# A Strassen scheme in the down projection of a two-layer convolutional MLP

## The reference

```python
D_FF = 2816
def conv_mlp(h, w_up, conv_w, conv_b, w_down):
    S = h.shape[1]
    u = h @ w_up
    up = jnp.pad(u, ((0, 0), (CONV_WIDTH - 1, 0), (0, 0)))
    uc = conv_b + sum(conv_w[j] * up[:, j:j + S] for j in range(CONV_WIDTH))
    gate, val = jnp.split(uc, 2, axis=-1)
    return (jax.nn.gelu(gate, approximate=True) * val) @ w_down
...
    for l in range(DEPTH):
        ...
        h = rms_norm(x, norm_mlp_pre[l])
        y = conv_mlp(h, w_up[l], conv_w[l], conv_b[l], w_down[l])
        x = x + rms_norm(y, norm_mlp_post[l])
```

## Time and profile before

| | |
|---|---|
| median of three runs | 3897.62 us |
| span of the profiled execution | 3899.6 us |
| TensorE matmul busy | 3734.7 us, 96% |
| VectorE busy | 2203.4 us, 57% |
| ScalarE busy | 1471.4 us, 38% |
| GpSimd busy | 1920.5 us, 49% |
| down projection of layer 0, first to last matmul | about 2468 to 2711 us |
| down projection of layer 1 | about 3649 to 3891 us |

### The profile page before, as it was taken

The page is one execution under the profiler, slowest core; times in us unless marked ns, Lnnn a source line. Parts: engine busy times, 40 slices in busy tenths (PEclk is TensorE's granted clock), DMA queues, the critical chain, the costliest instruction groups (busy, mean ns, idle before and its releaser), DMA issues.

```text
span 3899.6 us, 49530 instructions
## 1 busy us (share of the span) xinstructions
PE 3734.7 (96%) x19015; PEld 3088.3 (79%) x19015; DVE 2203.4 (57%) x3514; ACT 1471.4 (38%) x2954; POOL 1920.5 (49%) x1675
## 2 busy tenths in 40 slices
PE   6999999899999998999898999999999898999998
PEld 5888887887888877877687888887878587888887
DVE  4425254836777756544648777444444648777533
ACT  3224231326666653226544333222225534333211
POOL 3223223823333327221536888976221526778975
PEclk9999999999999999999899999999999999999999
DMA  5323222320000013110132222544110132222543
GB/s 182 96 83 92 81 67 85 107 78 15 6 12 6 9 37 102 61 30 7 33 131 78 81 84 79 200 145 138 49 36 17 33 125 73 84 84 87 180 161 124
DMA packets 244615, 309.84 MB, mean 79 GB/s; under 512 B 38085, under 2 KB 156245, under 8 KB 244378
## 3 DMA queue, kind: packets, MB, share of 16 engines
q1 hardware_dynamic: 211768, 231.86, 19.1%
q10 hardware_dynamic: 32610, 74.80, 5.5%
HBM read 252.96 MB, written 51.53 MB: 78 GB/s over the span
## 4 chain that ended last, share of the span: by engine, by line
PE 68%; DVE 12%; ACT 3%; issue 3%; POOL 1%; DMA 0%; ACTq 0%; SPq 0%; DVEq 0%; POOLq 0%
PE ps L130 64%; PE ps L133 3%; DVE ml_p L142 3%; DVE cst_sm L153 3%; ACT thi L136 1%; DVE f_ta L150 1%; DVE f_tb L150 1%; ACT ml_o L136 1%; DVE tlo L142 1%; ACT tfi L136 0%; POOL mlo_z L142 0%; DVE cst_sm L150 0%; DVE tfl L142 0%; POOL mix_z L142 0%; DMA wst<-in_w_in 0%
## 5 line engine op out<-in xcount | busy, mean ns | idle before, releaser
L139 POOL CAST whi<-wst 128x512 fp32r<-128x512 f32 (+2 forms) x508 | 423.9, 834 | 1241.2 <-DMA wst<-in_a_w_in 347.9
L142 POOL TENSOR_TENSOR wlo<-wst,whi 128x512 fp32r<-128x512 f32 (+2 forms) x634 | 936.2, 1484 | 40.8
L130 PE MATMUL ps<-whi,thi 128*128 128x512 f32 (+3 forms) x1816 | 710.1, 391 | 28.7 <-DVE tlo L142 10.8
L130 PE MATMUL ps<-whi,tlo 128*128 128x512 f32 (+3 forms) x1816 | 686.2, 378 | 0.0
L130 PE MATMUL ps<-wlo,thi 128*128 128x512 f32 (+3 forms) x1816 | 685.6, 378 | 0.0
L130 PEld LDWEIGHTS ps<-whi,thi 128*128 128x128 f32 x1816 | 345.2, 190 | 90.5 <-DVE tlo L142 11.9
L130 PEld LDWEIGHTS ps<-wlo,thi 128*128 128x128 f32 x1816 | 345.5, 190 | 57.7 <-issue 3.8
L130 PEld LDWEIGHTS ps<-whi,tlo 128*128 128x128 f32 x1816 | 344.6, 190 | 58.3
L130 PE MATMUL ps<-thi,whi 128*128 128x512 f32 x856 | 339.2, 396 | 23.2 <-DVE tlo L142 15.0
L130 PE MATMUL ps<-thi,wlo 128*128 128x512 f32 x856 | 336.0, 392 | 0.0
L130 PE MATMUL ps<-tlo,whi 128*128 128x512 f32 x856 | 335.9, 392 | 0.0
(11 more groups left out here) (393 smaller groups left out, 8103.9 us busy)
## 6 DMA issues: line engine op xcount, KB each, us to landing
wst<-in_w_down SPq DMA_DIRECT2D x140, 256.0 KB, 3.3
wst<-in_w_up SPq DMA_DIRECT2D x126, 256.0 KB, 2.9
scr_h<-f_tb SPq DMA_DIRECT2D x44, 512.0 KB, 3.9
wst<-in_w_in SPq DMA_DIRECT2D x80, 256.0 KB, 2.8
da_am<-in_ada_w SPq DMA_DIRECT2D x64, 256.0 KB, 2.7
wst<-in_a_w_in SPq DMA_DIRECT2D x72, 192.0 KB, 2.4
f_T2lw<-scr_h SPq DMA_DIRECT2D x48, 256.0 KB, 3.8
tfl<-scr_h SPq DMA_DIRECT2D x40, 256.0 KB, 3.8
```

The source lines that it names most:

```text
L130: return self.none if self.e is None else self.e.matmul(*a, **k)
L139: return self.none if self.e is None else self.e.tensor_copy(*a)
L142: return self.none if self.e is None else self.e.tensor_tensor(*a)
```

## The change

The down projection is cut in 2 x 2 x 2 blocks: two halves of the positions, two halves of the 22 feature tiles (tiles 2 to 12, and tiles 0, 1 and 13 to 21) and two halves of the columns. A Strassen scheme (the variant of Winograd) makes seven block products out of them. A product has 11 steps `e` of one contraction tile each, and a step covers four row tiles `t` with three matmuls each. That is 77 steps of 12 matmuls, 924 matmuls in a layer. Three products accumulate in the four banks of chain `y`, two in the banks of chain `x1` and two in those of `x2`; the intermediate values of a chain are read out between the products.

The sums of operands are new. In products 1, 2 and 4 each step needs a sum of hidden tiles and a sum of weight tiles. The hidden difference `S3` is made by VectorE during the up projection (`difference`) and stored to `d_s`. `S2` is made by GpSimd (`pool_down_sum`), four steps ahead. `T3`, `T2`, `T4`, `S4`, `T1` and `S1` are made by VectorE (`dve_down_sums`), four steps ahead too. Raw tiles that are needed more than once stay in kept tiles (`keep`: 11 each of `1`, `3`, `4` and `S`). ScalarE now makes all high parts, of weights too (`act_down`). GpSimd makes the low parts of all weights and those of the hidden tiles in `POOL_LOWS`; VectorE makes the other ones. Rows 0 to 3 end with product 5 and rows 4 to 7 with product 6, the last.

The core of the diff:

```diff
+    DOWN = [("A11", "B11", "x1"), ("S2", "T2", "y"), ("A12", "B21", "x1"), ("S3", "T3", "y"), ("S1", "T1", "x2"),
+            ("A22", "T4", "y"), ("S4", "B22", "x2")]
...
+    def down_h_free(self, l, e):
...
+        return self.S.at("tile", ("dw", l, e - 8))
...
+        for e in range(6, 12):
+            self.sp_feature(sp, l, e)
+        for i in range(4):
+            self.sp_keep(sp, l, "S", i)
+            self.sp_keep(sp, l, "S", i + 4)
+            self.sp_keep(sp, l, 4, 3 + 2 * i)
+            if i < 3:
+                self.sp_keep(sp, l, 4, 4 + 2 * i)
+        self.sp_hidden(sp, l, 21)
+        for i in range(3, 11):
+            self.sp_keep(sp, l, 3, i)
+            if i >= 8:
+                self.sp_keep(sp, l, "S", i)
+        self.sp_keep(sp, l, 4, 10)
+        for e in range(12, 77):
+            self.sp_feature(sp, l, e)
+            if e + 3 < 77:
+                self.sp_weight(sp, l, e + 3)
...
+    def sp_keep(self, sp, l, name, i):
...
+        elif name == 3:
+            sp.wait_ge(*(self.up_done(l, "A11") if i < 3 else S.at("g_mul", (l, 21)) if i < 9 else S.at("st_h", (l, 21))))
...
+        else:
+            sp.wait_ge(*(S.at("tile", ("dw", l, i % 4)) if i < 8 else S.at("g_mul", (l, 21))))
...
+        for e in range(77):
+            self.pool_down_sum(q, l, e + 4)
+            self.pool_down(q, l, e)
...
+    def pool_down_sum(self, q, l, e):
...
+        q.wait_ge(*S.at(self.down_h_sem(e), (l, e)))
+        x = self.keep["S"][i]
+        q.tensor_tensor(x, x, self.down_h(e)[2], ALU.subtract).then_inc(*S.up("p_seq", (l, "S2", i)))
...
-    STAGED = 18
+    STAGED = 4
...
+        for p in range(7):
...
+            for i in range(11 if p < 6 else self.STAGED):
+                for t in range(4):
+                    step(p, i, t)
+        for t in range(4):
+            for i in range(self.STAGED, 11):
+                step(6, i, t)
+            self.down_rows(self.pe_row, q, l, 4 + t)
...
+            if e in (17, 39):
+                self.act_down_out(q, l, e // 11 - 1)
+            if e == 74:
+                self.down_rows(self.act_row, q, l, 0)
+            if e > 74:
+                self.down_rows(self.act_row, q, l, e - 74)
+            self.act_down(q, l, e)
+        for t in range(3, 10):
             self.down_rows(self.act_row, q, l, t)
...
+    POOL_LOWS = [6, 7, 8, 9, 10, 13, 17, *(e for e in range(22, 33) if e % 3), *(e for e in range(44, 55) if e % 3), 74, 75, 76]
...
+        def difference(m):
...
+            q.tensor_tensor(self.s3, self.tb[:, half(1)], self.tb[:, half(0)], ALU.subtract).then_inc(*S.up("u_mid", (l, m, "D3")))
...
+        for e in range(6, 77):
+            if e in (28, 50, 61):
+                self.dve_down_out(q, l, {28: 1, 50: 3, 61: 4}[e])
+            if e == 74:
+                self.dve_down_out(q, l, 5)
+                self.down_rows(self.dve_row, q, l, 0)
+            if e > 74:
+                self.down_rows(self.dve_row, q, l, e - 74)
+            self.dve_down_sums(q, l, e + 4)
+            self.dve_down(q, l, e)
```

More of the change, by code:

```diff
@@ new lines, in pe_down, with step @@
+        for chain, ring in (("x1", "dx"), ("y", "dy")):
+            for t in range(4):
+                B.take(("dn", l, chain, t), ring)
+        def step(p, i, t):
+            e, chain = 11 * p + i, self.DOWN[p][2]
+            bank = B.of(("dn", l, chain, t))
+            q.wait_ge(*self.down_low_ready(l, e))
+            q.wait_ge(*S.at("w_lo", ("dw", l, e)))
+            if i == 0 and p in (0, 1, 4):
+                for event in B.freed(("dn", l, chain, t)):
+                    q.wait_ge(*event)
+            elif i == 0:
+                q.wait_ge(*(S.at("m1", (l, "down", t)) if p == 2 else S.at("u_mid", (l, {3: "U2", 5: "U3", 6: "C22"}[p], t))))
+            gh, gl, _ = self.down_h(e)
+            wh, wl, _ = self.wslot(self.down_slot(l, e))
+            c, first, last = blk(t), i == 0 and p in (0, 1, 4), i == 10
+            q.matmul(ps[:, bank, :], gh[:, c], wh, start=first, stop=False, skip_group_check=True)
+            q.matmul(ps[:, bank, :], gh[:, c], wl, start=False, stop=False, skip_group_check=True)
+            ins = q.matmul(ps[:, bank, :], gl[:, c], wh, start=False, stop=last, skip_group_check=True)
+            if last or t == 3:
+                ins.then_inc(*S.up("tile", ("dp", l, p, t) if last else ("dw", l, e)))
+            if last and t == 3:
+                S.also("tile", ("dw", l, e))
@@ new lines, in dve_down_out @@
+    def dve_down_out(self, q, l, p):
+        S, B, z = self.S, self.B, self.rows["f", l]["z"]
+        chain = self.DOWN[p][2]
+        for t in range(4):
+            q.wait_ge(*S.at("tile", ("dp", l, p, t)))
+            q.wait_ge(*S.at("m1", (l, "down", t)))
+            key = ("dn", l, chain, t)
+            out, add = {1: (z[:, 4 + t, half(1)], z[:, t, half(0)]), 3: (z[:, t, half(1)], z[:, t, half(0)]),
+                        4: (z[:, t, half(1)],) * 2, 5: (z[:, t, half(0)],) * 2, 6: (z[:, 4 + t, half(1)],) * 2}[p]
+            ins = q.tensor_tensor(out, self.ps[:, B.of(key), :], add, ALU.add)
+            if p < 5:
+                ins.then_inc(*S.up("u_mid", (l, {1: "U2", 3: "U3", 4: "C22"}[p], t)))
+            else:
+                ins.then_inc(*B.free(key, "evac_v"))
+                S.also("evac_v", (("fin", l), t, 1))
@@ L3247, in dve_mlp, with dve_down_end @@
+    def dve_down_end(self, q, l, t):
+        S, B, z = self.S, self.B, self.rows["f", l]["z"]
+        key = ("dn", l, "x2", t)
+        q.wait_ge(*S.at("tile", ("dp", l, 6, t)))
+        q.tensor_tensor(z[:, 4 + t, half(1)], self.ps[:, B.of(key), :], z[:, 4 + t, half(1)], ALU.add).then_inc(
+            *B.free(key, "evac_v"))
+        S.also("evac_v", (("fin", l), 4 + t, 1))
     def dve_mlp(self, q, l):
```

322 lines of the change are left out of this document (206 added, 116 removed).

## The result

The changed kernel takes 3942.7 us (median of four runs, 3940.7 to 3943.3) where the kernel before takes 3898.3 (four runs, 3896.6 to 3899.0). The ratio is 1.0114, with an interval of 1.0102 to 1.0127. The forecast was 3883 with a range up to 3908, so it is wrong in sign and the time lies out of its range. The profiled execution has a span of 3940.6 us against 3899.6.

A forecast was written before the change was run, and what follows sets the result against it. TensorE was taken as the bound, 0.227 us a matmul. Savings of 29.9 us a layer less waits gave -5.2 us in layer 0 and -9.6 in layer 1, together -14.8 from 3897.6: 3883 us, range 3855 to 3908.

The forecast's parts named there:

- bare saving: Both down projections: 132 fewer matmuls a layer at 0.227 us, 59.9 us in two layers if nothing waits.
- steps 18 to 65: Down projection: GpSimd over by 0.4 us in 11 steps, covered by a 4 us lead; 0, else 4 us a product.
- part of 32: Down projection, steps 8 to 17: TensorE waits for late loads and GpSimd's queued work, 16 us in either layer.
- part of 12.6: End of each down projection: last-product waits 3.8 and 1.6 us, tail 5 and 2.2 us, layers 0 and 1.
- there are 0.67 us of cover for 0.6 us: Up projection: the subtraction nearly hides before the read-out the product waits for; 0 to 0.1 us a block, 0.5 a layer.
- with the cover gone: Up projection: if the subtraction is not hidden, 0.6 us in each of 11 blocks, 6.6 us a layer.
- First wait: Down projection, steps 8 to 17: GpSimd waits for hidden tile 12, then 25 operations take 37 us; 16 us a layer.
- I take 2493 (2491 to 2496): Layer 0's down projection: the time in us at which hidden tile 12 lands, after which GpSimd's 25 operations begin.
- backlog of up to 3 us: Start of the down projection: loads for steps 1 to 3 ask 385 GB/s, so this much may stand ahead of tile 12.
- The rival of full exclusion: Down projection: each VectorE operation costs GpSimd its own 0.62 us, 10 us a layer more, 3903 us; chance 0.2.
- Rows and tail: End of down projection: waits of 3.8 and 1.6 us in product 6, tail 5 and 2.2 us, layers 0 and 1.
- The clock: the rival: Steps 8 to 17: gaps keep TensorE at half clock for ten steps, 36 us more in two layers, 3919; chance 0.12.

The follow-up runs named there:

- small difference: Changed kernel with VectorE's difference S3 made over 16 of its 512 columns in ten of eleven up projection blocks: 3933.2 us, ratio 1.0092.
- small sums: Changed kernel with VectorE's six sums in the down projection made over 16 of their 512 columns: 3908.7 us, ratio 1.0031.
- three at once: Changed kernel with VectorE's six sums and S3 made over 16 columns and the loads in order of need: 3874.3 us, ratio 0.9937.
- rows made small: On top of three at once, VectorE's scalings and addition of rows 0 to 3 over 16 of 1024 columns: 3853.2 us, ratio 0.9892.
- three or four changes together: Three at once; or the changed kernel with ordered loads, work moved to VectorE, new row order and later S3: 3874.7 us, ratio 0.9941.

## Why the prediction was wrong

The bare saving was right as counted: 59.9 us from 3897.7 is 3837.8, and the change stands 104.9 us above it, where the forecast allowed 45. The step that failed worst is the pricing of VectorE's new sums. The sum charged GpSimd 0.43 us for each operation of VectorE, and put at nothing what GpSimd costs VectorE and what the port costs in steps 18 to 65; the sums cost 34.0 us. The terms for the loads, the rows and `difference` were too small as well. Both layers together:

| what | forecast | measured | by |
|---|---|---|---|
| `difference` in the up projection | 1.0 | 9.5 | small difference |
| VectorE's sums beside GpSimd | part of 32 | 34.0 | small sums |
| late loads | part of 32 | 24.9 (argued) | three at once, less the two above |
| rows 0 to 3 | part of 12.6 | 21.1 | rows made small |
| not taken apart | | 15.4 | rest; 9.4 of it are gaps early in the stages |

**Up projection: wrong.** The step that failed is "there are 0.67 us of cover for 0.6 us". The 0.6 us was right for the operation itself. The cover was less. 0.14 us of it is not to be had, since the product starts that much behind the read-out in the chain. The real cover is the time by which `f_ub` comes sooner across the product: 6.99 us before (2213.45 to 2220.44), 6.57 after, so 0.42 us. And with the cover gone `f_ta` starts while GpSimd is still at work on the lows, another 0.39 us (3.22 for 2.83). VectorE is 0.99 us later against 0.42 of cover, and 0.57 is what a block grew by. The 6.6 us a layer that I gave for "with the cover gone" was near what came: 4.8 us by the small difference, 5.4 and 5.8 by the distances of the blocks.

**First wait: right in place and cause, too small.** Its first part failed: "I take 2493 (2491 to 2496)". Tile 12 was issued at 2494.42 and landed at about 2501. GpSimd's `S2` sum for it, and the chain's legs (the store, and the load of a neighbour issued 0.95 us behind tile 12):

```profile
2482.23 9.90 DMA scr_h<-f_tb
...
2495.37 6.80 DMA tfl<-scr_s
```

```profile
2501.04 1.26 POOL L142 TENSOR_TENSOR d_s<-d_s,tfl 128x512 f32<-128x512 f32 x1 [14.29 <-DMA tfl<-scr_s]
```

The store took 9.9 us against the 3.0 of the earlier trace rows, the load of tile 12 about 6.6 against 3.8. (It came from `scr_s`, where the differences are stored, not from `scr_h` as the prediction has it.) The DMA engines moved 391 GB/s in all of 2470 to 2500 us, as in the earlier trace rows, but what stood ahead of a load was more than the "backlog of up to 3 us": the `S` loads landed 8.3 us after their issue. A duration from a quiet stretch was used in a full one. The second part held: 37 us for GpSimd's 25 operations. The first began at 2501.04; this is the 25th, the low part of the hidden tile of step 17:

```profile
2537.60 1.74 POOL L142 TENSOR_TENSOR tlo<-d_s,thi 128x512 fp32r<-128x512 f32 x1
```

It ends 38.3 us after the first begins, and step 17 starts on TensorE at 2539.45. Without waits it would have been 2469.5 + 17 x 2.72 = 2515.7; the wait is 23.7 us for a forecast of 16, inside the bounds of 8 to 25. Tile 12 came 8 us later than the 2493 of the forecast, and that is nearly the whole difference.

**Steps 18 to 65: wrong.** I took 0 and gave "4 us a product" without the lead. It was missing, since step 17 started 0.1 us after its last operand, with nothing done ahead: 6.5 and 3.7 us of gaps in layer 0, and the slow clock on top. These gaps are ended by VectorE's low parts and not by GpSimd's, which the sum by GpSimd's operations could not show.

**The port: the wrong side was priced.** From the earlier trace rows I took what an operation of VectorE costs GpSimd, 0.43 us, and this was right (1.70 - 1.24 = 0.46). What GpSimd costs VectorE was never in the sum: its 0.6 us become 1.70. Three operations a step are then 5.1 us against 2.72; steps 19 and 20 took 5.08 and 5.06. It could be read in the kernel before: the low part that takes 0.69 us alone takes 0.90 beside GpSimd, and a little earlier 1.44:

```profile
2658.59 1.44 DVE L142 TENSOR_TENSOR f_T2l<-f_T2lw,f_T2h 128x512 fp32r<-128x512 f32 x1 [4.79 <-ACT f_T2h L136]
```

In the kernel before it did no harm, since VectorE was idle between its lows. The rival of full exclusion named the mechanism and had the same error: it charged GpSimd 0.62 instead of 0.43 us, VectorE nothing, and came to 10 us a layer more. The small sums give 17.

**Rows and tail: too small.** The waits for the last copies and low parts were 7.9 us in layer 0 and 5.8 in layer 1 for 3.8 and 1.6. I used 1.25 us for the addition of a row; it took 2.19, and GpSimd's two lows took 1.6 and 2.25 us. A row took 6.72 us. Both are the same port again, by their lengths; no run takes it away for the rows alone. The tail has no run of its own either: the 21.1 us are copies and tail together.

**The clock: the rival fell, though its wait came.** It said that ten steps would run at half clock. Behind the 13.9 us step 8 did (its matmuls stand 0.425 us apart, where full clock gives 0.227), then eight matmuls of step 13, and no other step up to 17: 4 us, as the granted 0.84 says, not 27. The gaps of 0.4 to 2 us in between did not keep the clock down. With these 4 us in it, the wait of 23.7 us is just past the 23.4 us from which the rival was to decide; what made the time was the rest. The forecast had the slow clock at nothing in its sum; in the two whole stages it came to about 20 us, spread over the rows of the table.

**What stays open.** Of the 15.4 us not taken apart, 5.0 and 4.4 us are gaps of TensorE in the first third of each stage in the run with three causes away, ended by GpSimd's lows and VectorE's. The other 6 have no experiment. The changed kernel is also 2.8 us ahead before layer 0's up projection (2114.0 for 2116.8) and gains 2.0 more between layer 0's down projection and layer 1's up projection, where the work is the same. The cause is open, and the stages themselves lost that much more than the times say. Why three or four changes together gave 11 us more than one by one was argued for the loads and not shown.

## What to carry to other kernels

Before work with two SBUF inputs is shared between VectorE and GpSimd, add up both engines' times as if they were one engine. Where that sum was over what a step takes, as here, giving nearly all of it to the faster engine was the better split. Price a DMA by what stands ahead of it at its own time, not by its duration in a quiet stretch, and look at what an in-order engine has queued behind the wait. Work that used to be hidden in the middle of a stage and now comes at its end has to be counted in full.

## What the runs showed of the hardware that was not expected

- A VectorE operation of 16 columns took 1.19 to 1.27 us beside a busy GpSimd, as long as one GpSimd operation of 512 columns (1.25).
- VectorE and GpSimd, both with work waiting, settled into turns of 1.70 us, GpSimd's 1.24 and VectorE's 0.46, over tens of microseconds at a time.
- An operation of VectorE put where VectorE was idle (2214.45 us) cost 0.27 us a block, by way of GpSimd.
- A store of 512 KB landed 9.9 us after its issue with the DMA engines full, 3.0 us in the kernel before.
